# Placing tokens for expert groups 2 to 7 earlier in a mixture-of-experts decoder layer

## The reference

```python
logits = (hf @ w_router + b_router).astype(jnp.float32)
top_val, top_idx = lax.top_k(logits, TOP_K)          # 4 of 32 experts for each token
wts = jax.nn.softmax(top_val, axis=-1)
...
gu = xb @ w_gu[e] + b_gu[e]                          # xb: the rows of the tokens of expert e
gt, up = gu[:, :D_FF], gu[:, D_FF:]                  # D_FF = 512
act = gt * jax.nn.sigmoid(SWIGLU_ALPHA * gt) * (up + 1.0)   # after clamps at 7
return act @ w_down[e] + b_down[e]
...
y = ys[dest] * w_sorted[:, None].astype(ys.dtype)
return jax.ops.segment_sum(y, tok, num_segments=n_tok).reshape(b_, L, D)
```

## Time and profile before

| | us |
|---|---|
| three timed runs | 967.42, 967.43, 968.34 |
| median | 967.43 |
| the profiled execution | 969.02 |
| its span, first to last instruction | 967.3 |
| TensorE busy | 934.3 (97%) |
| VectorE busy | 405.1 (42%) |
| ScalarE busy | 227.0 (23%) |
| GpSimd busy | 198.2 (20%) |
| mean granted TensorE clock | 0.995 |

### The profile page before, as it was taken

How to read it: one execution, slowest core, us unless ns; L and a number is a source line. 1 busy time by engine, 2 the same in 40 slices (tenths; PEclk the granted TensorE clock), 3 DMA queues, 4 the chain that set the end, 5 groups by cost and what they waited for, 6 DMA issues and landing times.

```text
span 967.3 us, 16928 instructions
## 1 busy us (share of the span) xinstructions
PE 934.3 (97%) x7147; PEld 495.7 (51%) x7147; DVE 405.1 (42%) x835; ACT 227.0 (23%) x488; POOL 198.2 (20%) x246
## 2 busy tenths in 40 slices
PE   3999999999999999999999999999999999999995
PEld 2676666657887657444444444444444444444442
DVE  0489977435534564145232232322323223232245
ACT  6334544452322232201011110111101111011112
POOL 2233941105100011123112111121111211111002
PEclk9999999999999999999999999999999999999998
DMA  9937546015426459999999999999999999999805
GB/s 323 364 102 260 188 162 250 11 53 180 143 78 261 184 200 401 315 367 402 332 379 392 385 393 392 389 404 380 396 391 384 403 384 395 385 393 400 325 10 187
DMA packets 71443, 283.96 MB, mean 294 GB/s; under 512 B 7488, under 2 KB 8796, under 8 KB 54984
## 3 DMA queue, kind: packets, MB, share of 16 engines
q1 hardware_dynamic: 61720, 257.93, 68.5%
q0 software_dynamic: 9648, 24.94, 9.6%
HBM read 272.62 MB, written 18.56 MB: 301 GB/s over the span
## 4 chain that ended last, share of the span: by engine, by line
PE 83%; DVE 9%; ACT 3%; DMA 3%; issue 1%; SPq 0%; POOLq 0%; POOL 0%; DVEq 0%; ACTq 0%
PE ps L1814 22%; PE ps L1528 15%; PE ps L1846 11%; PE ps L1825 11%; PE ps L1836 6%; PE ps L1763 2%; DVE small L1170 2%; PE ps L1801 2%; DVE top L1169 2%; PE ps L1582 2%; PE ps L1668 2%; PE ps L1913 2%; PE ps L1549 1%; PE ps L1809 1%; PE ps L1683 1%
## 5 line engine op out<-in xcount | busy, mean ns | idle before, releaser
L1357 DVE TENSOR_SCALAR mix<-ps 128x384 f32<-128x384 f32 x32 | 17.9, 558 | 345.8 <-ACT attn L1002 345.8
L1528 PE MATMUL ps<-h_hi,wb_hl 128*128 128x512 f32 x384 | 125.6, 400 | 0.0
L708 POOL DMA_INDIRECT moe_rows<-mix,ius x31 | 50.9, 1641 | 247.0 <-DVE mix L1406 136.5
L1002 ACT ACTIVATE attn<-ps 128x384 f32<-128x384 f32 x32 | 15.7, 491 | 308.6 <-PE ps L1825 308.6
L1528 PEld LDWEIGHTS ps<-h_hi,wb_hl 128*128 128x128 f32 x384 | 72.1, 188 | 20.8 <-issue 3.9
L1528 PE MATMUL ps<-h_lo,wb_hl 128*128 128x512 f32 x192 | 74.9, 390 | 0.0
L1398 DVE SCALAR_TENSOR_TENSOR mix<-ps,WC,attn 32x256 f32<-32x256 f32 x128 | 61.5, 481 | 7.2 <-PE ps L1836 4.9
L1406 DVE SCALAR_TENSOR_TENSOR mix<-ps,WC,attn 64x512 f32<-64x512 f32 x64 | 47.8, 747 | 34.5 <-PE ps L1846 33.5
L1814 PE MATMUL ps<-ring,mix 128*64 128x512 f32 x272 | 59.9, 592 | 0.0
L1814 PE MATMUL ps<-ring,uvp 128*64 128x512 f32 x256 | 58.6, 607 | 0.0
L1014 ACT ACTIVATE attn<-ps 128x384 f32<-128x384 f32 x32 | 15.7, 491 | 168.1 <-PE ps L1913 168.1
(11 more groups left out here) (311 smaller groups left out, 1503.1 us busy)
## 6 DMA issues: line engine op xcount, KB each, us to landing
ring<-in_w_gu_dram SPq DMA_DIRECT2D x66, 1024.0 KB, 15.3
ring<-in_w_down_dram SPq DMA_DIRECT2D x30, 1024.0 KB, 10.8
ring<-in_w_ada_dram SPq DMA_DIRECT2D x12, 2048.0 KB, 12.0
area_b<-in_w_gu_dram SPq DMA_DIRECT2D x16, 1024.0 KB, 14.5
hT<-in_w_gu_dram SPq DMA_DIRECT2D x16, 1024.0 KB, 15.8
X<-in_w_gu_dram SPq DMA_DIRECT2D x16, 1024.0 KB, 15.1
area_a<-in_w_gu_dram SPq DMA_DIRECT2D x14, 1024.0 KB, 16.0
ring<-in_w_in_dram SPq DMA_DIRECT2D x6, 2048.0 KB, 8.9
```

The source lines that it names most:

```text
L708: pool.indirect_dma_start(out=y_dram, in_=Y[0:slots, b, :], in_offset=None, out_offset=bass.IndirectOffsetOnAxis(ap=which, axis=0), bounds ...
L1528: last = mm(out_, a, b, start=(n == 0 and start_), stop=(n == len(pairs) - 1))
```

## The change

Groups 2 and 3 are moved to expert 0: VectorE compares them after its wait for `g2` and before `gated(0)`, and TensorE computes their places after expert 0's up-projection. Groups 4 and 5 go to expert 1, groups 6 and 7 to expert 2, and the indices of groups 2 to 7 are computed after expert 2. On TensorE the places of a period now stand ahead of the transposes of the next expert's rows (`rows(e + 1)`, for the experts 0 and 1).

```diff
-        LATE_GROUPS = {1: (2,), 2: (3,), 3: (4, 5), 4: (6, 7)}
+        LATE_GROUPS = {0: (2, 3), 1: (4, 5), 2: (6, 7)}
@@ VectorE
             dve.wait_ge(g2_in, 16)
+            for g in LATE_GROUPS[0]:
+                one_hot(g)
             gated(0)
             expert(1, 1, reused=False, groups=LATE_GROUPS[1])
             expert(2, 0, reused=False, groups=LATE_GROUPS[2])
-            expert(3, 1, groups=LATE_GROUPS[3])
-            expert(4, 0, groups=LATE_GROUPS[4])
             dve.wait_ge(oh_used, NE // OHE)
             token_rows(bank("ix", 1)[:, 3 * OHE:], 2 * OHE, NE - 2 * OHE).then_inc(idx_ok, 1)
-            for e in range(5, NE - 1):
+            for e in range(3, NE - 1):
                 expert(e, e % 2)
@@ TensorE
                 if e:
                     pe.wait_ge(xg_ok, e + 1)
                     up(e)
+                for g in groups:
+                    places(g)
                 if e < 2:
                     rows(e + 1)
-                for g in groups:
-                    places(g)
                 if e:
```

## The result

The changed kernel takes 970.2 us (median of 20 runs, 967.6 to 972.5), the kernel before 968.22 us in runs beside it (20 runs, 967.2 to 970.0). The ratio is 1.0016 with a 95% interval of 1.0010 to 1.0023: 1.6 us slower, between 1.0 and 2.2.

The account below looks back on a forecast made before the run. TensorE, busy 97% of the span, was taken to bound the kernel. Places -1.90, hold +3.0 and clock 0 gave +1.1 us on 967.43: 968.5 us, own range 967.6 to 969.3, whole range 965.4 to 970.2.

Parts of the forecast that it names:

- rival B: TensorE before expert 1: GpSimd held, longer idle stretch, low clock for more of the up-projection; up to 970.2 us, chance 0.20.
- Step 1: TensorE, experts 1 to 4: places of groups 2 and 3 move into expert 0's wait, -1.90 us.
- The +0.45 for the order: TensorE: places ahead of expert 1's row transposes start its up-projection 0.45 us later; dropped if the gathers land 3.0 us later.
- Step 2: VectorE's pair of one-hots holds GpSimd's index copy and first gathers at the head of the chain, +3.0 us.
- GpSimd isn't let in between the two either: A GpSimd instruction beside a pair of one-hots waits until both are through; read from a scatter of 3.87 us.
- I take no change: Flight time of the later gathers stays as before (gather 0: 8.21 us); bounds -2.4 and +2.6 us.
- as much: Gather 1, queued behind gather 0 on GpSimd, lands 3.0 us later too.
- Step 3: TensorE's clock fall at expert 1's up-projection costs the same 1.70 us as before: change 0, between -1.15 and +1.70.
- Step 4: GpSimd's later index waits, gathers and first scatter, and SyncE's loads: all have slack or move along, 0 us.
- signs: Expected in the trace: copy or gather 0 3 us long, gather 0 landing near 395.1, periods 19.0, 17.3, 17.3 from expert 2.

Follow-up runs that it names:

- the slot numbers in PSUM: Changed kernel, with the one-hots of groups 2 and 3 reading a copy of the slot numbers in PSUM instead of SBUF: ratio 0.9980, 966.08 us.
- the same filled: Changed kernel with 20 idle matmuls, whose results nothing reads, in expert 0's wait on TensorE: ratio 0.9991, 967.52 us.
- the hold filled: Kernel before, one-hots of groups 2 and 3 repeated ahead of expert 0's activation, 24 idle matmuls in TensorE's wait: ratio 1.0017, 969.45 us.
- the hold alone: Kernel before, with the one-hots of groups 2 and 3 done once more ahead of expert 0's activation, no places moved: ratio 1.0030, 970.53 us.
- the changed kernel once more: Changed kernel with nothing altered, a second profiled execution: 968.28 us.

## Why the prediction was nearly right, and where it was off

The forecast of +1.1 us stands beside a measured +1.6 (1.0 to 2.2). The median forecast, 968.5, lies 1.7 under the 970.2: 0.5 is this difference, and 0.8 is the kernel before itself, whose median over 20 runs is 968.22 and not the 967.43 of three; the rest is that medians and the ratio of all runs differ a little. As a time 970.2 is the upper edge of the range and the value of rival B, and lies above the forecast's own range of 967.6 to 969.3.

- **Step 1** held. The periods are 19.00, 17.33, 17.33, and the stretch with the slot numbers in PSUM is 470.83 - 382.69 = 88.14 us, 1.6 us below the kernel before without a fall (89.73). The +0.45 for the order, which the sum had dropped beside the hold, didn't show without the hold either: expert 1's up-projection starts 14.34 us after the first index operation there, 14.38 and 14.08 in the two traces of the kernel before.
- **Step 2** had the right mechanism and too large a size. Forecast was +3.0 for gather 0, whichever of copy and pair starts first. By ScalarE's copy of the weights it is +2.0, +1.7 and +1.2 in the three traces where the pair starts first (the changed kernel, the same filled, the hold filled), and +0.9 and +0.6 in the two where the copy does (the hold alone, the changed kernel once more). Two things make it less. The part that failed is "GpSimd isn't let in between the two either". It rested on scatters; a scatter is again held through both in the changed kernel (3.89 us at 421.68), but an index copy or a gather got in after the first one-hot in all six traces with the pair beside them at the head of the chain. And "I take no change" for the flight failed: gather 0's issue ends 2.4 us later than before in all three held traces, counted from the first index operation, but its rows land only 2.0 to 1.2 later. For gather 1 "as much" was taken, and it is +1.3 in the first trace.
- **Step 3** failed. I took 0 for the clock, since the trace showed a fall that the kernel before already paid for; its second trace doesn't have it. Filling gains 0.6 us in the kernel before and 2.4 us in the changed kernel. The clock's share of the change is about +1.8 us (the intervals of the three ratios allow about 1.4 us either way), and the granted clocks of the timed runs give as much. It is rival B's mechanism, in part of the executions.
- The two errors have opposite signs: 1.0 or more too much for the hold, 1.8 too little for the clock. That the sum came near is luck: -1.9 + 2.0 + 1.8 = 1.9 us, and with the lowest of the held traces 1.1.
- **Step 4** held: no wait on GpSimd's later gathers shows on TensorE, whose periods are the bare 17.33 us.
- Of the **signs** named, the places came as forecast, but index copy and gather 0 were 1.70 and 2.28 us long, not 3, and gather 0's weights were read at 394.15 by the clock of the trace before, not 395.1. Expert 1's up-projection started at 398.06, or 398.89 by that clock, close above the 398.5 below which the prediction was to be wrong; in the second trace of the changed kernel (397.88, or 397.16 by that clock) it is below. By its own sign, then, the +3.0 of step 2 did not hold up.

## What to carry to other kernels

An engine that is free for 11 us is not a place that is free: look at what GpSimd does in those microseconds, and whether it starts a chain; if it does, an operand in PSUM, or a start behind GpSimd's instructions, takes VectorE out of its way. A saving in matmul work that is paid for with a wait in front of TensorE is paid twice when the wait lets the clock fall. And a term read from one execution (here the fall of the clock) should be seen in a second one before it is called the state of the kernel.

## What the runs showed of the hardware that I had not expected

A one-hot with one input in PSUM takes as long (3.42 us the pair) and leaves GpSimd alone. A GpSimd instruction held by a pair of VectorE instructions can get in between the two: at the head of the chain three index copies (1.70, 1.75, 1.70 us) and three gathers (2.51, 2.12, 1.94 us) did, while a scatter beside a pair took 3.86 to 3.89 us in every trace; why they differ isn't shown. A semaphore raised by GpSimd's queue behind a gather rose before the gather had done its work, in the one trace that has it (the pair started at 386.06, gather 1 at 386.18); one raised by a copy behind it rose after (gather 1 through at 386.94, the pair from 387.23).
